# Two engines for the remainders of a projection's input: odd tiles on GpSimd, even tiles on VectorE

## The reference

```python
# block 1: three mixers of width 512, one output matrix
y = jnp.concatenate([y_hg, y_gla, y_ml], axis=-1).astype(x.dtype)
x = x + y @ w_out[l]
# block 2
y_a = jnp.einsum('bsc,cd->bsd', u, w_conv_proj[l])
y_b = jnp.einsum('bsc,cd->bsd', o, w_ret_proj[l])
m = jax.nn.sigmoid(g_a) * y_a + jax.nn.sigmoid(g_b) * y_b
x = x + jnp.einsum('bsd,de->bse', m, w_out[l])
# block 3
merged = g_sb * (y_sb @ w_out_sb) + g_ssd * (y_ssd @ w_out_ssd) + g_rw * (y_rw @ w_out_rw)
return x + merged @ w_o
```

## Time and profile before

| | |
|---|---|
| median of 3 runs | 6171.3 us (6171.18 to 6187.53) |
| span of the profiled execution, first to last instruction | 6168.7 us |
| TensorE matmul busy | 5304.3 us (86%) |
| VectorE busy | 2356.5 us (38%) |
| ScalarE busy | 1048.2 us (17%) |
| GpSimd busy | 734.1 us (12%) |
| mean granted clock of TensorE | 0.897 of 2.4 GHz |

### The profile page before, as it was taken

One profiled execution on the slowest core, in us unless ns is written; L12 is line 12 of the kernel. 1 busy time (PEld: TensorE's weight loads), 2 busy tenths in 40 slices (PEclk: granted clock), 3 DMA queues, 4 the chain that ended last, 5 costly groups with the idle time before them and its releaser, 6 DMA issues. The chain is left out here.

```text
span 6168.7 us, 56392 instructions
## 1 busy us (share of the span) xinstructions
PE 5304.3 (86%) x22484; PEld 3616.5 (59%) x22484; DVE 2356.5 (38%) x2465; ACT 1048.2 (17%) x1110; POOL 734.1 (12%) x386
## 2 busy tenths in 40 slices
PE   6999899665899999886788799999999899998977
PEld 4665466443678778665566365574756644454455
DVE  3333433455221221499543321313122234445643
ACT  1212111101111111111011211212111122222211
POOL 0000000000212212243222010000101000010011
PEclk8999899756899999998899899979888899998988
DMA  2110111201111111111221101101000121112321
GB/s 79 34 34 20 45 55 62 92 24 41 58 55 41 62 55 41 65 34 55 89 102 38 65 27 35 35 28 34 28 21 28 35 75 51 38 61 96 123 92 55
DMA packets 100373, 325.36 MB, mean 53 GB/s; under 512 B 10413, under 2 KB 20157, under 8 KB 100074
## 3 DMA queue, kind: packets, MB, share of 16 engines
q1 hardware_dynamic: 83498, 262.00, 12.9%
q10 hardware_dynamic: 16704, 60.82, 2.4%
HBM read 249.21 MB, written 73.58 MB: 52 GB/s over the span
## 5 line engine op out<-in xcount | busy, mean ns | idle before, releaser
L228 PE MATMUL ps<-b_hT,rw_fill_w 128*128 128x512 f32 x896 | 424.8, 615 | 9.9 <-ACT rw_fill_out L249 9.9
L465 PE MATMUL ps<-b_hi,ret_w_hi 128*128 128x512 f32 x768 | 303.8, 396 | 57.7 <-DVE ret_w_lo L432 29.6
L465 PE MATMUL ps<-b_lo,ret_w_hi 128*128 128x512 f32 x768 | 300.9, 392 | 0.0
L228 PEld LDWEIGHTS ps<-b_hT,rw_fill_w 128*128 128x128 f32 x896 | 168.3, 199 | 184.3 <-issue 169.6
L228 PE MATMUL ps<-b_hT,sb_xz_w 128*128 128x512 f32 x512 | 244.7, 622 | 10.3 <-DMA sb_xz_w<-in_w 10.3
L465 PE MATMUL ps<-b_hi,ret_w_lo 128*128 128x512 f32 x768 | 238.4, 392 | 0.0
L132 PE MATMUL ps<-b_hT,rw_w 128*128 128x512 f32 x512 | 225.0, 602 | 15.4 <-DVE rws_y L2769 15.4
L1572 DVE SCALAR_TENSOR_TENSOR xT<-b_pads,cols_sb,xT 128x1024 f32 (+1 forms) x134 | 213.2, 1607 | 0.0
L465 PE MATMUL ps<-b_hi,conv_w_hi 128*128 128x512 f32 x384 | 154.2, 401 | 63.9 <-ACT conv_sg L1619 44.5
L132 PE MATMUL ps<-b_hT,hg_w 128*128 128x512 f32 x384 | 175.3, 618 | 39.1 <-DVE b_y L887 21.8
L2664 POOL TENSOR_TENSOR rw_al<-rw_at,b_level_mask 128x1024 f32<-128x1024 f32 x24 | 56.4, 2351 | 1255.6 <-DVE rw_ak L2732 1152.3
(11 more groups left out here) (698 smaller groups left out, 10776.1 us busy)
## 6 DMA issues: line engine op xcount, KB each, us to landing
ret_w<-in_w SPq DMA_DIRECT2D x64, 512.0 KB, 3.5
rw_fill_w<-in_w SPq DMA_DIRECT2D x32, 512.0 KB, 3.8
conv_w<-in_w SPq DMA_DIRECT2D x24, 512.0 KB, 3.5
hg_w<-in_w SPq DMA_DIRECT2D x16, 512.0 KB, 3.6
gla_fill_w<-in_w SPq DMA_DIRECT2D x16, 512.0 KB, 3.6
scratch_ml_park<-gla_fill_out ACTq DMA_DIRECT2D x16, 512.0 KB, 3.5
scratch_x_park<-xT SPq DMA_DIRECT2D x16, 512.0 KB, 4.9
scratch_gate_park<-ret_gates_out ACTq DMA_DIRECT2D x16, 512.0 KB, 2.6
```

What stands on the lines that cost most here:

```text
L228: ins = pe.matmul(self.out[:, lo:lo + 512], w[:, k * P:k * P + P], h[:, k, lo:lo + 512], start=(k == 0), stop=(k == KD - 1))
L465: ins = pe.matmul(out[:, t], w, y, start=start, stop=stop)
```

## The change

`cut_y` takes a first tile and a stride. In the nine stages (`shared=True`) GpSimd cuts y tiles 1, 3, 5, 7 (or 1, 3), ahead of the weights in its program, and counts them in a semaphore of its own, `y_cut_pool`; VectorE cuts the even ones. Who waits for tile k (TensorE, and SP in ya and yssd) waits for the semaphore of that tile. convend and cnorm keep one engine.

```diff
-    def __init__(self, st, y, nk, ring, halves=None):
+    def __init__(self, st, y, nk, ring, halves=None, shared=False):
...
+        self.y_cutters = 2 if shared else 1
+        self.y_cut_pool = st.sem("y_cut_pool") if shared else None
...
-    def cut_y(self, eng):
-        for k in range(self.nk):
+    def y_cut_of(self, k):
+
+        return (self.y_cut, self.y_cut_pool)[k % self.y_cutters], k // self.y_cutters + 1
+
+    def cut_y(self, eng, first=0):
+        for k in range(first, self.nk, self.y_cutters):
             eng.wait_ge(self.y_rounded, k + 1)
             eng.tensor_tensor(self.y_lo[:, k, :], self.y[:, k % self.y.shape[1], :], self.y_hi[:, k, :], ALU.subtract) \
-                .then_inc(self.y_cut, 1)
+                .then_inc(self.y_cut_of(k)[0], 1)
...
-                pe.wait_ge(self.y_cut, k + 1)
+                pe.wait_ge(*self.y_cut_of(k))
...
-        self.proj, self.added = SplitProjection(st, y, nk, 2, halves), st.sem("added")
+        self.proj, self.added = SplitProjection(st, y, nk, 2, halves, shared=True), st.sem("added")
...
     def cut_weights(self, pool):
+        self.proj.cut_y(pool, 1)
         self.proj.cut_weights(pool, KD)
...
-        proj = SplitProjection(st, y, nk, 2, halves)
+        proj = SplitProjection(st, y, nk, 2, halves, shared=True)
...
-                    sp.wait_ge(proj.y_cut, k + 1)
+                    sp.wait_ge(*proj.y_cut_of(k))
...
+            proj.cut_y(pool, 1)
             proj.cut_weights(pool, KD)
```

## The result

The changed kernel takes 6207.1 us, the median of 20 runs (6180.8 to 6221.2), the kernel before beside it 6183.3 (20 runs, 6171.2 to 6198.5): a ratio of 1.0033 [1.0023, 1.0043]. A second set gave 6202.5 against 6191.0, 1.0014 [0.9999, 1.0029]. Over all runs of the two sets the change stands at a mean of 6201.6 (32 runs), the kernel before at 6186.3 (159 runs, those beside the experiments included): 15 us more, with an uncertainty of some 5. The two sets by themselves differ in their means by 21.5 and 8.6 us. So it is slower by about 0.25%, and 6207.1 lies above the predicted range, which ended at 6190.0.

The account below looks back on a forecast made before the run. TensorE was taken as the bound, so only its waits in the changed stages count. 6168.7 + 8.6 of stalls + 1.7 of clock = 6179.0, with 2.6 for the median 6181.6 us; range 6173.0 to 6190.0.

Parts of the forecast that it names:

- Parts 1 to 3: Changed stages: subtractions take turns, y ends later, weight tile 1 queues behind them; 2.1 us per eight-tile stage, 8.6 in all.
- S: In each changed stage, the start of VectorE's subtraction of y tile 0, from which times are counted.
- small stalls at tiles 5 and 7: Stages with eight y tiles: TensorE waits 0 to 0.5 us before these y tiles; first output tile no later within 0.1.
- fall: TensorE's clock dropping after the stall at the second output tile; 1.7 us each, one in the four stages likeliest.
- no turns: Rival: VectorE's and GpSimd's subtractions run beside each other, TensorE's waits at tile 2 go; 6167.7 us, chance 0.05.
- Part 4: ya and yssd: weight tile 2, behind SP's parked-x loads, comes about 1.2 us later but costs nothing, with 2.7 us cover.
- Part 5: Long stages: a stall of 2.0 us may also lower TensorE's clock; +1.7 us likeliest, none and four drops the ends.
- the sum: Whole kernel: 8.6 us of stalls and 1.7 of clock added to 6168.7, giving 6179.0, seen as 6181.6.
- The base of the sum: Whole kernel before: span of 6168.7 us in the profiled execution, with the median of runs 2.6 us over it.
- Same or slower: Whole kernel: verdict by a bound of 0.3%, 18.5 us; same 0.94, slower 0.05, faster 0.01.

Follow-up runs that it names:

- four tiles: The change only in the five stages with four y tiles, against the kernel before: 6177.0 us, ratio 0.9993.
- late pair: The change only in yssd and o3, behind the rwkv scan, against the kernel before: 6180.6 us, ratio 0.9998.
- the five delays: Kernel before with added VectorE subtractions ahead of block 3, 1.4, 2.6, 3.8, 5.0 or 6.2 us: 6200.1, 6185.5, 6187.3, 6204.2, 6185.8 us.
- waiting weights: Kernel before, but GpSimd waits with its first weight tile until VectorE has cut all of y: 6193.4 us, ratio 1.0005.
- early: The change only in ya and o2, ahead of the rwkv scan, against the kernel before: 6198.7 us, ratio 1.001.
- two dense kernels: Kernel before with four or two additional 128x512 matmuls, their results unused, in each step of the rwkv scan: 6149.5 and 6136.8 us.

## Why the prediction was right or wrong

**Parts 1 to 3, the mechanism: right.** The turns are 3.33 us where 3.31 was worked out; the last y cut ends at S+13.48 (13.39), the second output tile starts at S+17.0 in all four stages (17.0). VectorE's second subtraction takes 2.85 us and not 3.3, as GpSimd's first starts at S+0.8, beside the one before. The small stalls at tiles 5 and 7 are there in yssd and o3 alone, 0.1 to 0.3 us; ya and o2 have none. TensorE waits 1.67 to 1.82 us at the second output tile (2.0). A stage without a fall costs 2.2 (2.1). Of the short stages yrw costs 0.3 (0.2) and ysb nothing; o1b and o1c vary more from one profile to the next than they could cost. The rival "no turns" is out, by VectorE's median of 3.13 us beside GpSimd.

**Part 4, SP's queue: right.** GpSimd takes weight tile 2 up at 3194.18, S+19.2, sooner than the 21.7 worked out and before TensorE needs it.

**Part 5, the clock: right in kind, a little small.** Two falls of 1.65 us each (1.7) in the profile after where one was taken as likeliest; in all profiles with the change 8 of 22 long stages fell, 1.5 in four. By that share the stages cost 4 x 2.2 + 1.5 x 1.65 = 11.3 us against 10.3 in the sum, and 11.7 in the profile after, inside the bounds of zero to two falls (8.6 to 12.0). The prediction named part 5 as the one that is wrong if the time is over 6190; the windows of the stages say that it isn't.

**The base of the sum: wrong, and this is the step of the prediction that failed.** "6168.7 of the profiled execution" and "the median of the runs is 2.6 us over that span" took one execution with unit 0 at short steps, and three runs (6171.18 to 6187.53), as the kernel's time, and put what the clock does outside the changed stages at nothing. The measured 6207.1 is 25.5 us over the 6181.6 of the sum. About 12 of these are the base: the kernel before took 6183.3 beside it. The other 13.6 are in the difference, 23.9 instead of 10.3, of which the stages' own cost explains about 1: in that set 10 of the 20 runs before were under 6184 us, and 3 of the 20 after under 6195, so one median stands at the edge of the low times and the other far from it. The profiles show the same: the span after is 22.2 us over the 6179.0 of the sum, 1.4 of it from the stages, 24.1 from the rwkv stage, -3.3 from all else.

Over 159 runs the kernel before has a mean of 6186.3, 15 us above 6171.3. From there the sum gives 6186.3 + 10.3 = 6196.6, and with 11.3 us of stages 6197.6, against a mean of 6201.6; the rest, 4.0, is inside the uncertainty of some 5. The profile of before had this: the scan's windows, the same instructions at granted clock 1.00 in unit 0 and 0.50 in unit 1, steps of 6.8 us in three units, and one of the three runs 16 us above the other two. Neither was read, as the change touches nothing there.

**Same or slower: not well placed.** With the stages' cost at 11.3 us, under the bound of 18.5, "same" was what the mechanism said. The first comparison gave 1.0033, just over 0.3%, the second 1.0014. How far a median over 20 or 12 runs moves when a few executions more or less have short steps was not in the chances.

**What stays open** is whether the change also makes the short steps rarer. The kernels with the change, or part of it, in ya and o2 show low times (under 6184 us, plus what the kernel's own edit costs) in about 16 of 78 runs, the kernel before in 69 of 159, and the others that leave ya and o2 alone (four tiles, late pair, the five delays, waiting weights) in 39 of 95. If executions are independent, so few of 78 come by chance in under one case of 1000, so the count speaks for a link. But the bound was chosen with the times in sight; the one sharp comparison, early against late pair, is 3 of 12 against 7 of 11 by this bound; and the delays have no simple order, so by what way the change would act on the scan isn't shown. A share of low times lower by 0.22, at some 20 us between low and high, is 4 to 5 us: as much as lies between 11.3 and 15.

## What to carry to other kernels

Here two-input work moved from VectorE to GpSimd didn't run in parallel with what stayed: look in the trace for one such instruction beside one of the other engine and add up durations before you count on a second engine, and ask what is queued behind the moved work. Before adding a difference to a base, look whether the base is one number: take more than three runs, and look in windows for the same instructions at two clocks, which make a spread that any change will seem to cause. A stretch of small dependent matmuls at half the clock may be worth more than anything that is moved between idle engines; a few large matmuls beside it raised the clock here.

## What the runs showed of the hardware

- VectorE and GpSimd took turns for the whole length of their two-input 128x1024 float32 subtractions: 1.21 and 2.39 us alone, up to 3.42 and 3.39 beside each other, a pair every 3.33 us. GpSimd's rounding (one input) was stretched too: 1.04 us alone, 2.05 beside a VectorE subtraction.
- In unit 1 of the scan before, TensorE has a matmul in flight for 33.00 of 35.00 us and is granted 1.2 GHz; with four matmuls of 512 columns more in each step it has one for 23.06 of 25.00 us, nearly the same share, and is granted 2.4 GHz.
- Which of the two a unit gets can differ from one execution to the next of the same program: 4.1 or 6.8 us a step, 6166 or 6213 us in the end.

The Trainium skill (page TensorE: Matmul & The Clock Gate, section Part 1: The HAM clock gate) says that the gate sets the clock by how busy TensorE has been of late, and that the number of matmuls that one kernel runs at the low clock at its start can differ from run to run. By the two dense kernels more work does raise the clock, so the trace agrees in direction; but the busy share as the profile shows it doesn't tell the two apart: it is 94% in unit 1 before at half the clock, 91% in unit 0 before and 92% in unit 1 with four matmuls, both at full.
